# Two transformer blocks in fp32: the end of the expert stage rearranged (products of the return, the exit of the branch, the last norms, the output transfers)

## The chip, the cores and the metric

One core of one Trainium2 chip runs the whole program. The metric is the device time of one execution in microseconds (us); the figure for a kernel is the median of its runs. A profile is one further execution with its trace. In the trace PE is TensorE (matmuls), PEld its weight loads, DVE VectorE, ACT ScalarE, SP the engine that issues the transfers.

## The reference, cut to what matters

256 tokens of width 1024 go through a first block (two layers of attention) and a second block (two layers, l = 0 and 1, each attention plus a mixture of 16 experts). The change touches only the end of the second block's layers:

```python
N_EXPERTS, N_GROUPS, TOP_K, D_EXPERT = 16, 4, 2, 256
def moe_ffn(x, w_router, router_bias, w_gate, w_up, w_down):
    ...                                          # each token picks a group of 4 experts and 2 experts in it
    h = jax.nn.silu(jnp.einsum('nd,edf->enf', xt, w_gate)) * jnp.einsum('nd,edf->enf', xt, w_up)
    h = h * gates.T.astype(h.dtype)[:, :, None]
    y = jnp.einsum('enf,efd->nd', h, w_down)

def second_block(x, ...):
    for l in range(DEPTH):                       # DEPTH = 2
        h = jnp.einsum('bsd,dc->bsc', x, w_in[l])
        ...                                      # three kinds of attention, w_out, first layer_norm
        x = layer_norm(DEEPNORM_ALPHA * x + moe_ffn(x, ...), ln2_g[l], ln2_b[l])
    return x
```

## The kernel before

Everything is float32. A product of full precision is made of three matmuls in fp32r (`mm3`, L485 to L489): high by high, low by high, high by low part. ACT makes the high part of each quarter of weights (`act_cut`, L432) and DVE the low part (`dve_cut`, L440), in turn with their other work; SP loads the weights through a ring (L422). Each engine's instructions stand in the order in which `pe_...`, `act_...`, `dve_...`, `sp_...` functions write them, by hand; engines wait for each other by semaphores (`wait_ge`), which hold up all that stands behind them on the same engine.

**The experts.** The tokens lie in two tiles of 128 (i = 0, 1). If no group of experts has more than 128 tokens, a branch taken by PE, DVE, ACT and SP alike (`branch`, a compare and a jump) runs `pe_few`, `act_few`, `dve_few`; otherwise the `all` way stands behind it, over which a taken jump leads at the end. In the trace the `few` way ran in both layers. It gathers the tokens of each group g into 128 rows (xg), runs for e = 0 to 15 the products with gate and up weights (24 matmuls), the turn of the hidden rows (`turned`, 2 transposes) and the products with the down weights (`down`, 12 matmuls: first and second quarter k_, and in each the output halves n = 0 and 1, 3 matmuls each). Four experts of a group sum in banks 2*(g%2)+n; then ACT writes the high part of the group's output (`ys`, L2323, two halves) and DVE the low part (L2373). `back(i, g0, g1)` brings the rows of groups g0 to g1 back to the tokens of tile i: for each half n and each group two matmuls (L2263) of the one-hot matrix OHT with the high and the low part of ys. In program order PE does: up(15) with turned(14) inside, down(14), turned(15), `back(0, 1, 3)` (8 matmuls), down(15), `back(0, 3, 4)` (4), `back(1, 0, 4)` (16). `back(0, 0, 1)` stands before up(15).

**The end of a layer.** `dve_added` (L1583) adds the banks to X by halves and sums; L1584 makes the mean, `dve_middle` (L1590) the centred product with the gain, ACT the squares (L1607) and a first root by LN and EXP (L675, L676), `dve_root` (L681 to L685) refines it, `dve_scaled` (L1598) writes X. All this is done for tile 0 and then for tile 1. In layer 1 SP then writes out each tile with one transfer (L2210). In layer 0 PE transposes X of tile 0 (`pe_flip_x`, L1616, 8 transposes) still inside the branch, ACT (L1622) and DVE (L1628) write its high and low part hT; behind the branch PE starts the projection h10 of layer 1 tile by tile (`pe_proj_by_tiles`): 18 matmuls of tile 0, the transposes of X of tile 1, 6 more of tile 0, then 24 of tile 1. ACT and DVE, behind their own jump, first cut one more quarter of weights and then write hT of tile 1.

`att_bank` deals out PSUM banks 4 to 7 in rotation. `pe_idle(n, b)` (L496) issues n matmuls with a zero operand.

Of the kernel before, what the change touches and what calls it, by code (L numbers as in the profile page):

```python
# [125 lines left out]
def program(nc, t, out, cols, keep):  # L126
# [254 lines left out]
    first_turned, second_normed = sem("first_turned"), sem("second_normed")  # L381
# [13 lines left out]
    def write(pe, act, dve, pool, sp, branch):  # L395
# [1183 lines left out]
        def dve_added(i, key, ready):  # L1579
            sums, mean = small(2, "sums", i, *key), small(1, "mean", i, *key)  # L1580
            for c, x in enumerate(in_two(X[:, i, :])):
                dve.wait_ge(ready[c])
                dve.e.scalar_tensor_tensor(x, x, ALPHA, banks[2 * i + c].t[:, :], MUL, ADD, accum_out=sums[:, c:c + 1]).then_inc(*dve.did("added", *key, i, c))  # L1583
# [9 lines left out]
        def dve_scaled(i, key):  # L1593
# [16 lines left out]
        def pe_flip_x(i, name, src, ready):  # L1610
            for c, j0 in enumerate((0, 4)):
                b = att_bank(("xT", name, i, j0), (first_turned, c + 1) if name in (("few", 0), ("all", 0)) else at("xT", name, i, j0))
# [12 lines left out]
        def dve_flip_x(i, name):  # L1625
            for j0 in (0, 4):
                dve.wait_ge(at("high", "xT", name, i, j0))
                dve.e.tensor_tensor(hT[1][:, j0:j0 + 4, i * P:(i + 1) * P], bank_of["xT", name, i, j0].t[:, :].rearrange("p (j n) -> p j n", j=4),  # L1628
                                    hT[0][:, j0:j0 + 4, i * P:(i + 1) * P].bitcast(F32), SUB).then_inc(
                    *((first_turned, 1) if name in (("few", 0), ("all", 0)) else dve.did("xT", name, i, j0)))  # L1630
# [45 lines left out]
        def pe_mix_layer(l):  # L1676
            second = [at("added", "o1", 1, c) if l == 0 else (second_normed, c + 1) for c in range(2)]
# [386 lines left out]
        def pe_all(l):  # L2064
# [44 lines left out]
            pe_finish(l, way)  # L2109
# [78 lines left out]
        def pe_finish(l, way):  # L2188
            if l == 0:
                pe_flip_x(0, way, X, [at("x", *way, 0, c) for c in range(2)])  # L2190

        def act_finish(l, way):
            for i in range(2):
                act_add_and_norm(i, way)
                if l == 0 and i == 0:
                    act_flip_x(0, way)

        def dve_finish(l, way, ready):
            for i in range(2):
                dve_added(i, way, ready[i])  # L2200
                dve_middle(i, way, ln_loaded(l, 2))
                dve_scaled(i, way)
                if l == 0 and i == 0:
                    dve_flip_x(0, way)

        def sp_finish(l, way):
            if l == 1:
                for i in range(2):
                    sp.wait_ge(*[at("x", *way, i, c) for c in range(2)])
                    sp.e.dma_start(out[0, i * P:(i + 1) * P, :], X[:, i, :]).then_inc(d_out, 16)  # L2210
# [3 lines left out]
        def pe_few(l):  # L2214
# [23 lines left out]
            def down(e):  # L2238
                g, x = e // 4, e % 2
                for k_ in range(2):  # L2240
                    w = pe_quarter()
                    pe.wait_ge(at(*way, "gh", e))
                    for n in range(2):
                        b = banks[2 * (g % 2) + n]
                        first = e % 4 == 0 and k_ == 0
                        if first:
# [3 lines left out]
                                 first, e % 4 == 3 and k_ == 1)  # L2250
                    mm.then_inc(w_used, 1)
# [231 lines left out]
```

## Time and profile before

| | us |
|---|---|
| median of 3 runs | 1190.86 (1190.43 to 1192.14) |
| the profiled execution, its own time | 1189.19 |
| its span, first to last instruction | 1187.8 |
| PE busy in the span | 1120.8 (94%) |
| DVE busy / ACT busy | 901.4 (76%) / 737.3 (62%) |
| mean granted clock of TensorE | 0.983 |

The page of the profile counts each engine's busy time; the chain of work that ended last says which engine's work the end waited for. Times in the timeline are from the start of the span. The end of layer 0 lies at about 866 to 896 us, that of layer 1 at 1166 to 1187.8 us. A clock of 1.00 is 2.4 GHz, 0.50 is 1.2 GHz.

### The profile page before, as it was taken

How to read it: one execution, taken by the hardware profiler on the slowest of the kernel's cores; microseconds unless marked ns; L12 is line 12 of the kernel's file. 1: busy time of each engine (PE TensorE's matmuls, PEld its weight loads, DVE VectorE, ACT ScalarE, POOL GpSimd, SP SyncE). 2: the span in 40 equal slices, each digit the busy share in tenths (PEclk: the TensorE clock that was granted, in tenths of full speed). 3: DMA queues.
4: the chain of work that ended last, by engine and by line, in shares of the span. 5: the costliest groups of instructions: out<-in, count | busy, mean ns of one | idle time of the engine just before them, and what ended most of it. 6: DMA issues, size and time to landing. Idle time of an engine off the chain costs nothing.

```text
span 1187.8 us, 14609 instructions
## 1 busy us (share of the span) xinstructions
PE 1120.8 (94%) x5487; PEld 916.0 (77%) x5487; DVE 901.4 (76%) x1474; ACT 737.3 (62%) x1307; POOL 0.2 (0%) x4
## 2 busy tenths in 40 slices
PE   7799999999988999999999999999989999999996
PEld 5688887788777788878777777877768778787774
DVE  4756757677667867766578868999977886899996
ACT  5645565655556666566355554888845555488883
POOL 0000000000000000000000000000000000000000
PEclk9999999999999999998999998999989999999999
DMA  8554454443433455532542415999926331499991
GB/s 297 188 210 142 142 178 154 139 168 107 154 130 107 149 206 169 198 106 95 189 143 105 141 51 164 341 362 361 360 79 235 107 129 49 150 341 356 366 344 39
DMA packets 131554, 221.26 MB, mean 186 GB/s; under 512 B 6112, under 2 KB 77328, under 8 KB 131472
## 3 DMA queue, kind: packets, MB, share of 16 engines
q1 hardware_dynamic: 127632, 213.21, 52.7%
q10 hardware_dynamic: 3840, 6.98, 1.7%
q8 instruction: 47, 0.77, 0.3%
q14 instruction: 35, 0.29, 0.1%
HBM read 219.13 MB, written 1.05 MB: 185 GB/s over the span
## 4 chain that ended last, share of the span: by engine, by line
PE 75%; DVE 12%; ACT 8%; issue 3%; DMA 2%; DVEq 0%; ACTq 0%
PE bank L487 20%; PE bank L489 20%; PE bank L488 20%; PE bank L849 3%; PE bank L784 2%; ACT wH L432 2%; DVE wL L440 2%; ACT S L804 2%; PE bank L636 1%; DMA ring<-in_w_mem_kv 1%; DVE mx L793 1%; PE bank L830 1%; PE bank L2221 1%; PE bank L1765 1%; PE bank L1698 1%
## 5 line engine op out<-in xcount | busy, mean ns | idle before, releaser
L440 DVE TENSOR_TENSOR wL<-ring,wH 128x1024 fp32r<-128x1024 f32 (+1 forms) x316 | 375.5, 1213 | 143.6 <-ACT wH L432 142.7
L432 ACT ACTIVATE wH<-ring 128x1024 fp32r<-128x1024 f32 (+1 forms) x316 | 320.3, 1047 | 30.3 <-PE bank L489 14.9
L487 PE MATMUL bank<-wH,hTH 128*128 128x512 f32 (+2 forms) x592 | 238.8, 403 | 6.8 <-issue 3.0
L488 PE MATMUL bank<-wL,hTH 128*128 128x512 f32 (+2 forms) x592 | 232.6, 393 | 0.0
L489 PE MATMUL bank<-wH,hTL 128*128 128x512 f32 (+2 forms) x592 | 232.4, 393 | 0.0
L487 PEld LDWEIGHTS bank<-wH,hTH 128*128 128x128 f32 x592 | 112.1, 189 | 32.0 <-issue 5.6
L489 PEld LDWEIGHTS bank<-wH,hTL 128*128 128x128 f32 x592 | 111.8, 189 | 24.9
L488 PEld LDWEIGHTS bank<-wL,hTH 128*128 128x128 f32 x592 | 112.1, 189 | 23.1 <-issue 0.5
L487 PE MATMUL bank<-wH,xgH 128*128 128x512 f32 x256 | 104.7, 409 | 0.0
L488 PE MATMUL bank<-wL,xgH 128*128 128x512 f32 x256 | 101.2, 396 | 0.0
L489 PE MATMUL bank<-wH,xgL 128*128 128x512 f32 x256 | 101.2, 395 | 0.0
L804 ACT ACTIVATE S<-bank,sm 128x256 f32<-128x256 f32 (+1 forms) x144 | 59.5, 428 | 62.4 <-DVE sm L797 62.2
L487 PEld LDWEIGHTS bank<-wH,xgH 128*128 128x128 f32 x256 | 48.1, 188 | 12.1 <-DVE wL L440 2.6
L555 ACT ACTIVATE qkv<-bank,factors 128x512 f32<-128x512 f32 x50 | 33.6, 689 | 38.0 <-PE bank L489 37.9
L489 PEld LDWEIGHTS bank<-wH,xgL 128*128 128x128 f32 x256 | 48.1, 188 | 11.5
L488 PEld LDWEIGHTS bank<-wL,xgH 128*128 128x128 f32 x256 | 48.2, 188 | 9.5
L487 PE MATMUL bank<-wH,gh 128*128 128x512 f32 x128 | 51.1, 399 | 0.1
L488 PE MATMUL bank<-wL,gh 128*128 128x512 f32 x128 | 50.6, 395 | 0.0
L489 PE MATMUL bank<-wH,gh 128*128 128x512 f32 x128 | 50.6, 395 | 0.0
L440 DVE TENSOR_TENSOR wL<-ring_G,wH 128x1024 fp32r<-128x1024 f32 x40 | 48.5, 1221 | 1.3 <-ACT wH L432 1.0
L440 DVE TENSOR_TENSOR wL<-ring_K,wH 128x1024 fp32r<-128x1024 f32 x40 | 48.3, 1219 | 1.5 <-ACT wH L432 1.4
L836 ACT ACTIVATE PT<-bank 128x512 f32<-128x512 f32 x44 | 25.4, 599 | 33.3 <-PE bank L830 33.3
(292 smaller groups left out, 1868.3 us busy)
## 6 DMA issues: line engine op xcount, KB each, us to landing
ring<-in_w_in_a SPq DMA_DIRECT2D x44, 1024.0 KB, 5.1
ring<-in_w_out SPq DMA_DIRECT2D x20, 1024.0 KB, 4.9
ring<-in_w_down SPq DMA_DIRECT2D x20, 1024.0 KB, 6.3
ring<-in_w_gate SPq DMA_DIRECT2D x36, 512.0 KB, 5.2
ring<-in_w_up SPq DMA_DIRECT2D x36, 512.0 KB, 6.7
ring<-in_w_in_b SPq DMA_DIRECT2D x14, 1024.0 KB, 5.1
ring<-in_w_mem_kv SPq DMA_DIRECT2D x8, 1024.0 KB, 7.0
ring<-in_w_in SPq DMA_DIRECT2D x8, 1024.0 KB, 5.5
```

The lines of the kernel that those rows point to most:

```text
L432: act.e.activation(quarter_parts(q)[0], quarter_in_ring(q), COPY).then_inc(w_high, 1)
L440: dve.e.tensor_tensor(lo, quarter_in_ring(q), hi.bitcast(F32), SUB).then_inc(w_low, 1)
L487: pe.e.matmul(o, a[0], b[0], start=first, stop=False)
L488: pe.e.matmul(o, a[0], b[1], start=False, stop=False)
L489: return pe.e.matmul(o, a[1], b[0], start=False, stop=last)
L555: act.e.activation(dst(i), bank_of["proj", name, i].t[:, 0:slab_w[name]], COPY, scale=factor(key)[:, i:i + 1] if key else 1.0).then_inc(*a ...
L636: tr = pe.e.transpose(o, src(i, j), ident)
L784: mm = pe.e.matmul(score_bank(u, s // each)[:, s % each, :], u.qh(s)[:, i * P:(i + 1) * P], u.kh(s)[:, k:k + n], start=u.mask is None, sto ...
L793: dve.follow().tensor_reduce(u.mx[:, each * x:each * x + each], score_bank(u, x), AX, MAX).then_inc(*dve.did())
L804: act.e.activation(u.S[:, s, 0:n], score_bank(u, s // each)[:, s % each, :], EXP, bias=nb[:, s:s + 1], scale=u.scale, accum_out=u.den[:, s ...
L836: act.e.activation(u.PT[:, kt, :, :].rearrange("p h q -> p (h q)"), bank_of["turn", u.name, kt].t[:, :], COPY).then_inc(*act.did("PT", u.n ...
L849: mm = pe.e.matmul(b.t[:, s * u.dv:(s + 1) * u.dv], u.PT[:, kt, s, :], u.vh(s, kt), start=kt == 0, stop=kt == u.nk - 1)
```

## The change

1. In `pe_few` tile 1 no longer uses banks 2 and 3, which hold the sums of group 3, but two banks of the rotation (6 and 7, which `turn["att"] = 3` at e = 15 arranges). So `back(1, ...)` is cut up: `back(1, 0, 2)` (8 matmuls) ahead of turned(15), `back(1, 2, 3)` (4) behind down(15), `back(0, 3, 4)` and `back(1, 3, 4)` (4 each) after it.
2. The last group of matmuls for half n = 0 of down(15) signals ("first half"), and ACT starts on that half of ys before the other one is done. The matmul with the high part of ys waits for ACT alone (`ys_high`), the one with the low part for DVE.
3. In layer 0 PE ends its branch with 10 matmuls by zero and transposes X of tile 0 behind the jump. Since both ways of the branch use it, it waits for a new semaphore `first_normed`. The same work of ACT and DVE stays inside the branch.
4. In layer 1 DVE adds both tiles, then does both middles, one refinement of the root with two columns, and four scalings; ACT does the squares of both tiles and one LN and EXP.
5. The output goes out in four transfers of a half tile (256 KB) instead of two of a tile (512 KB).

```diff
-                if key[-1] == 0 and i == 1:
-                    mm.then_inc(second_normed, 1)
+                if key[-1] == 0:
+                    mm.then_inc((first_normed, second_normed)[i], 1)
...
         def pe_mix_layer(l):
+            if l:
+                turn["att"] = 3
+                pe_flip_x(0, "exit", X, [(first_normed, 1), (first_normed, 2)])
...
-        def pe_finish(l, way):
-            if l == 0:
-                pe_flip_x(0, way, X, [at("x", *way, 0, c) for c in range(2)])
         def act_finish(l, way):
+            if l:
+                ss = small(2, "ss2", *way)
+                for i in range(2):
+                    act.wait_ge(at("mean", i, *way))
+                    act.follow().activation(squares[:, :], X[:, i, :], SQUARE, bias=small(1, "mean", i, *way), accum_out=ss[:, i:i + 1]).then_inc(*act.did("sum", "ln", *way))
+                act_root(("ln", *way), ss, 2, 1.0 / D, "eps5")
+                return
...
+        def dve_finish(l, way, ready, sums_in=(None, None)):
+            if l:
+                for i in range(2):
+                    dve_added(i, way, ready[i], sums_in[i])
+                for i in range(2):
+                    dve_middle(i, way, ln_loaded(l, 2))
+                dve.wait_ge(at("sum", "ln", *way))
+                r = dve_root(("ln", *way), small(2, "ss2", *way), 2, 1.0 / D, "eps5")
+                ...
+                return
...
-                    sp.e.dma_start(out[0, i * P:(i + 1) * P, :], X[:, i, :]).then_inc(d_out, 16)
+                    for c in range(2):
+                        sp.wait_ge(at("x", *way, i, c))
+                        sp.e.dma_start(out[0, i * P:(i + 1) * P, c * 512:(c + 1) * 512], X[:, i, c * 512:(c + 1) * 512]).then_inc(d_out, 16)
...
+                        if e == 15 and k_ == 1 and n == 0:
+                            mm.then_inc(*pe.did(*way, "first half", e))
...
             def back(i, g0, g1):
                 for n in range(2):
-                    b = banks[2 * i + n]
                     if g0 == 0:
-                        pe.wait_ge(b.free, at(*way, "OHT", i))
-                        b.free = at("added", *way, i, n)
+                        if i:
+                            b = att_bank((*way, "back", 1, n), at("added", *way, i, n))
+                        else:
+                            b = bank_of[(*way, "back", 0, n)] = banks[n]
+                            ...
...
-                        pe.wait_ge(at(*way, "ys", g, n))
                         for x in range(2):
+                            pe.wait_ge(at(*way, "ys" if x else "ys_high", g, n))
...
+                if e == 15:
+                    back(1, 0, 2)
             turned(15)
             back(0, 1, 3)
             down(15)
+            back(1, 2, 3)
             back(0, 3, 4)
-            back(1, 0, 4)
-            pe_finish(l, way)
+            back(1, 3, 4)
+            if l == 0:
+                pe_idle(10, att_bank((*way, "idle"), None))
```

PE from the end of down(14) to turned(15) in layer 0, of before: ys_137 to ys_140 are groups 1 and 2, T_67 the hidden rows.

```order
L489 MATMUL bank<-wH_102,gh_144 128x512
L2235 MATMUL bank<-const,T_67 128x128 x2
L2263 MATMUL bank<-ys_137,OHT 128x512
L2263 MATMUL bank<-ys_138,OHT 128x512
L2263 MATMUL bank<-ys_139,OHT 128x512
```

And of after, where ys_135 and ys_136 are group 0:

```order
L489 MATMUL bank<-wH_102,gh_144 128x512
L2301 MATMUL bank<-ys_135,OHT 128x512
L2301 MATMUL bank<-ys_136,OHT 128x512
L2301 MATMUL bank<-ys_137,OHT 128x512
L2301 MATMUL bank<-ys_138,OHT 128x512
L2301 MATMUL bank<-ys_135,OHT 128x512
L2301 MATMUL bank<-ys_136,OHT 128x512
L2301 MATMUL bank<-ys_137,OHT 128x512
L2301 MATMUL bank<-ys_138,OHT 128x512
L2266 MATMUL bank<-const,T_67 128x128 x2
```

Eight matmuls for tile 1 moved ahead of turned(15), so ahead of down(15) too. DVE at the end of layer 1, of before:

```order
L1583 SCALAR_TENSOR_TENSOR X,sm<-X,bank 128x512 x2
L1584 TENSOR_SCALAR sm<-sm 128x1
L1590 SCALAR_TENSOR_TENSOR middle_86<-X,sm,lnw 128x512 x2
L681 TENSOR_SCALAR sm<-sm 128x1
L683 SCALAR_TENSOR_TENSOR sm<-sm 128x1
L684 TENSOR_TENSOR sm<-sm 128x1
L685 SCALAR_TENSOR_TENSOR sm<-sm 128x1
L1598 SCALAR_TENSOR_TENSOR X<-middle_86,sm,lnw 128x512 x2
```

and the same eight once more for tile 1. Of after, for both tiles:

```order
L1583 SCALAR_TENSOR_TENSOR X,sm<-X,bank 128x512 x2
L1584 TENSOR_SCALAR sm<-sm 128x1
L1590 SCALAR_TENSOR_TENSOR middle_86<-X,sm,lnw 128x512 x2
L1590 SCALAR_TENSOR_TENSOR middle_87<-X,sm,lnw 128x512 x2
L681 TENSOR_SCALAR sm<-sm 128x2
L683 SCALAR_TENSOR_TENSOR sm<-sm 128x2
L684 TENSOR_TENSOR sm<-sm 128x2
L685 SCALAR_TENSOR_TENSOR sm<-sm 128x2
L2227 SCALAR_TENSOR_TENSOR X<-middle_86,sm,lnw 128x512 x2
L2227 SCALAR_TENSOR_TENSOR X<-middle_87,sm,lnw 128x512 x2
```

where L1583 and L1584 stand twice ahead of the middles; four instructions of one column went.

## Rows read from the trace of the kernel before

**Rows 1.** Page, part 4: shares of the span on the last chain, by engine

```profile
PE 75%; DVE 12%; ACT 8%; issue 3%; DMA 2%; DVEq 0%; ACTq 0%
```

**Rows 2.** Chain that ended last, end of layer 1: start us, us, what

```profile
1166.51 1.86 PE bank L2263 x8
...
1171.21 0.61 ACT ys L2323
1171.84 0.70 DVE ys L2373
...
1172.58 0.74 PE bank L2263 x2
...
1173.35 1.31 DVE X L1583 x4
...
1177.36 1.42 DVE X L1598 x2
1178.78 1.22 DVE X L1583 x4
...
1180.27 1.43 DVE middle L1590 x2
```

**Rows 3.** Timeline, end of layer 1: start us, us, engine, line

```profile
1172.58 4.98 PE L2263 MATMUL bank<-ys,OHT 128*128 128x512 f32 x20 [1.41 <-DVE ys L2373]
...
1178.85 5.83 SPq L2210 DMA_DIRECT2D out<-X  x2
...
1182.84 1.41 DVE L1598 SCALAR_TENSOR_TENSOR X<-middle,sm,lnw 128x512 f32<-128x512 f32 x2
```

**Rows 4.** DMA issues, 1170 to 1188 us: KB each, median us to landing

```profile
out<-X SPq DMA_DIRECT2D x2, 512.0 KB, 3.0
```

**Rows 5.** Timeline, layer 0, around the start of down(15)

```profile
866.99 2.11 PE L2263 MATMUL bank<-ys,OHT 128*128 128x512 f32 x8
...
868.60 0.42 DVE L2362 TENSOR_TENSOR gh<-bank,gh 128x256 fp32r<-128x256 f32 x1
...
869.17 0.47 PE L487 MATMUL bank<-wH,gh 128*128 128x512 f32 x1
```

**Rows 6.** Timeline, layer 0, across the exit of the branch

```profile
879.19 1.32 PE L1616 MATMUL bank<-const,X 128*128 128x128 f32 x8 [0.63 <-DVE X L1598]
...
883.52 0.69 PE L487 MATMUL bank<-wH,hTH 128*128 128x416 f32 x1 [3.02 <-issue]
...
887.61 0.90 ACT L432 ACTIVATE wH<-ring 128x832 fp32r<-128x832 f32 x1 [2.45 <-issue]
...
888.76 1.03 DVE L440 TENSOR_TENSOR wL<-ring,wH 128x832 fp32r<-128x832 f32 x1 [1.57 <-ACT wH L432]
...
889.20 1.03 PE L1616 MATMUL bank<-const,X 128*128 128x128 f32 x8
...
890.46 1.29 DVE L1628 TENSOR_TENSOR hTL<-bank,hTH 128x512 fp32r<-128x512 f32 x2 [0.68 <-ACT hTH L1622]
...
891.21 0.46 PE L487 MATMUL bank<-wH,hTH 128*128 128x416 f32 x1
...
895.86 0.37 PE L487 MATMUL bank<-wH,hTH 128*128 128x452 f32 x1
```

**Rows 7.** Busy time by stretch: us, busy of each engine, granted clock, DMA share, GB/s

```profile
882.00:889.00 7.00, 5.48 (x17) 5.29 (x18) 4.99 (x14) 2.64 (x5) 0.00 (x0) 0.55 0.03 6
...
1005.00:1014.00 9.00, 9.00 (x34) 7.67 (x34) 5.29 (x18) 4.38 (x7) 0.00 (x0) 0.50 0.18 73
```

**Rows 8.** Queues of the transfers, 880 to 882 us: packets, MB, share of 16 engines

```profile
q8 instruction: 1, 0.02, 3.6%
```

**Rows 9.** Timeline, entry of layer 0's branch: zero products and what follows

```profile
716.31 3.76 PE L496 MATMUL bank<-zeroR,identR 128*128 128x512 f32 x8
...
717.02 0.14 DVE L2038 CAST count<-sm 1x1 int32<-1x1 f32 x1
...
719.86 2.35 PE L2221 MATMUL bank<-OH,xs 128*128 128x512 f32 x7
```

More of the change, by code:

```diff
@@ L1611, in pe_flip_x @@
             for c, j0 in enumerate((0, 4)):
-                b = att_bank(("xT", name, i, j0), (first_turned, c + 1) if name in (("few", 0), ("all", 0)) else at("xT", name, i, j0))
+                b = att_bank(("xT", name, i, j0), (first_turned, c + 1) if name == "exit" else at("xT", name, i, j0))
                 pe.wait_ge(ready[c])
@@ L1628, in dve_flip_x, with act_flip_exit, dve_flip_exit @@
                 dve.e.tensor_tensor(hT[1][:, j0:j0 + 4, i * P:(i + 1) * P], bank_of["xT", name, i, j0].t[:, :].rearrange("p (j n) -> p j n", j=4),
-                                    hT[0][:, j0:j0 + 4, i * P:(i + 1) * P].bitcast(F32), SUB).then_inc(
-                    *((first_turned, 1) if name in (("few", 0), ("all", 0)) else dve.did("xT", name, i, j0)))
+                                    hT[0][:, j0:j0 + 4, i * P:(i + 1) * P].bitcast(F32), SUB).then_inc(*dve.did("xT", name, i, j0))
+        def act_flip_exit(way):
+            for j0 in (0, 4):
+                act.wait_ge(at("turned", "xT", "exit", 0, j0))
+                act.e.activation(hT[0][:, j0:j0 + 4, 0:P], bank_of["xT", "exit", 0, j0].t[:, :].rearrange("p (j n) -> p j n", j=4),
+                                 COPY).then_inc(*act.did("high", "exit", way, j0))
+        def dve_flip_exit(way):
+            for j0 in (0, 4):
+                dve.wait_ge(at("high", "exit", way, j0))
+                dve.e.tensor_tensor(hT[1][:, j0:j0 + 4, 0:P], bank_of["xT", "exit", 0, j0].t[:, :].rearrange("p (j n) -> p j n", j=4),
+                                    hT[0][:, j0:j0 + 4, 0:P].bitcast(F32), SUB).then_inc(first_turned, 1)
         def dve_rotate(src, dst, n, w, c, s, *name, scratch=T0):
@@ L2320, in down @@
                     g = e // 4
-                    act.wait_ge(at(*way, "down", e), at(*way, "gathered", 7))
+                    act.wait_ge(at(*way, "gathered", 7))
                     for n in range(2):
+                        act.wait_ge(at(*way, "first half", e) if e == 15 and n == 0 else at(*way, "down", e))
                         act.e.activation(ys[g][0][:, n * 512:(n + 1) * 512], banks[2 * (g % 2) + n].t[:, :], COPY).then_inc(*act.did(*way, "ys_high", g, n))
@@ L2393, in dve_few @@
             down(15)
-            dve_finish(l, way, [[at(*way, "back", i, n) for n in range(2)] for i in range(2)])
+            dve_finish(l, way, [[at(*way, "back", i, n) for n in range(2)] for i in range(2)],
+                       [[bank_of[(*way, "back", i, n)] for n in range(2)] for i in range(2)])
         def experts(l):
```

31 lines of the change are left out of this document (19 added, 12 removed).

## The prediction, written before the changed kernel ran

> **What bounds the kernel.** I read the page's shares of the last chain first: the end waits for PE in three quarters of the span [rows 1]. Next the chain by time around the two ends of a layer, since the change touches nothing else: there the work that is waited for goes from PE over ACT and DVE to DVE alone [rows 2]. Last the timeline of those places, for what lies beside the chain.
>
> Three readings carry the rest. (a) In the last expert PE has no gap: eight products of the return fill 1.86 us of the chain, ahead of down(15) [rows 2]. (b) Behind down(15) PE is not what the end waits for. Its 20 products run from 1172.58 to 1177.56 [rows 3], but DVE adds tile 1 only at 1178.78, when it is through with tile 0 [rows 2]. (c) In layer 0 PE starts h10 at 883.52, 3.02 us after its last transpose, with nothing to wait for but its jump [rows 6]. Yet the 24 products of tile 1 wait for hT of tile 1, whose first low part DVE writes from 890.46 on; they start at 891.21 [rows 6].
>
> **Part 1, products pulled ahead.** Eight products of tile 1 come from behind down(15), where PE had time (b), to a place ahead of it, where it has none (a). Price in layer 1: +1.86 us on everything behind. In layer 0 down(15) started at 869.17, while the eight products ahead of it, begun at 866.99, were issued by 868.85; the 0.32 between was a wait for DVE's low part of the hidden rows, 868.60 to 869.02 [rows 5]. That wait is covered now, as its inputs move by 1.86 too but DVE is free sooner than that: +1.86 - 0.32 = +1.54. What it buys is that tile 1 is ready for DVE soon after tile 0, which only part 4 uses.
>
> **Part 2, the half signal.** Before, ACT started at the end of the last product (1171.21), DVE 0.63 later, PE at 1172.58, DVE's add at 1173.35, that is 2.14 us in all [rows 2]. Now half n = 0 is signalled three products earlier, 3 x 0.233 (1.86 / 8) = 0.70. ACT's first half is over when the last product ends, DVE's low part of it 0.65 later. ACT's second half cannot start before that last product, so DVE's second low part ends at 1.31 + 0.04. PE meanwhile issues back(1, 2, 3), four products, until 0.76; its pair for half 0 goes at 0.76 and 0.99, and the add, which followed the pair's start by 0.77 before [rows 2], can start at 1.5. Gain 2.14 - 1.5 = 0.65 us in either layer. If ACT or DVE were not free then, the gain would be 0; in layer 0 they have two more quarters of weights to cut, but these end at about 872.3 and the half signal comes at 873.0.
>
> So the first add moves by +1.86 - 0.65 = +1.2 in layer 1 and +1.54 - 0.65 = +0.9 in layer 0.
>
> **Part 3, the exit of layer 0.** PE's last real product now starts at about 873.7 + 2.4 = 876.1 (last expert's end 872.2 + 1.54, then the pairs above and four more). Ten zero products at 0.25 (4.98 / 20, [rows 3]) last to 878.7. X of tile 0 is there at 879.19 + 0.9 = 880.1. The jump cost at least the 3.02 us of PE's idle time and at most 883.52 - 879.85 = 3.6, counted from the start of the last four transposes. At 880.75 the trace has one packet of 16 KB on a queue named instruction [rows 8]: PE fetches code. If the jump is taken while the zero products still run, PE is back by 876.2 + 3.6 = 879.8, in time. For that speaks the entry of layer 0: the count was written at 717.16, zero products ran from 716.31 to 720.07, and the first product of the branch followed at 719.86 with no gap, with PE's reading of the count and its branch between [rows 9]. Value taken: 0, bounds 0 and +1.9 (878.7 + 3.3 - 880.1, jump behind the last zero product).
> The Trainium skill ("Runtime: NRT & Kernel Launch", Instruction fetch mechanics) says that a taken branch to a target outside the fetched window stalls until the page is brought; the trace's 16 KB packet and the 3 us agree. Its "Advanced Engine Details and Errata" (Engine Queue Depths) gives TensorE a queue of 64: by that all zero products fit behind one another and the jump is reached in time; without such a queue the sum would be 1.9 us higher.
>
> What does PE's earlier start bring? h10 starts when the first low part of tile 0 is there, 881.2 + 0.9 = 882.1 instead of 883.52, and perhaps at full clock: from 882 to 889 the granted clock was 0.55 [rows 7], after PE had stood still. But both are hidden. Tile 1's products wait for DVE, and DVE for ACT: ACT comes out of its own jump at 887.61, cuts a quarter (0.90), DVE cuts it at 888.76 (1.03), and only then writes hT [rows 6]. ACT's jump follows the last root of tile 1, which moved by +0.9. So ACT is back at 888.5, DVE's cut starts at 889.65 and ends at 890.7, and tile 1's low part starts there instead of 890.46. Before, 0.67 us went between DVE's cut and its low part on PE's late transposes (889.20) and ACT; now X of tile 1 is turned by 889. Sum for layer 0: +0.9 - 0.67 = **+0.2**. If the cover by ACT were not there, PE's gain of 1.4 would show.
>
> **Part 4, one root for both tiles.** From the first add to the end of the last scaling DVE took 1173.35 to 1184.25 = 10.9 us, that is per tile 1.49 for add and mean, 1.43 middle, 1.1 root, 1.42 scaling [rows 2, 3]. Now the root stands once (-1.1), and its ACT part is over while DVE does the four middles (-0.2), with 0.1 less where like instructions follow each other. Tile 1's banks are ready at about 2.9 after down(15), its first add comes at 3.0: no wait. Gain **1.4**, bounds 1.1 and 1.6.
>
> **Part 5, output by halves.** The last transfer was 512 KB and landed 3.0 us after issue [rows 4]. The last one is now 256 KB; at some 410 GB/s its data take 0.64 us less, and the three ahead of it are issued 0.7 us apart, as DVE's scalings end. Issue by SP takes some 0.4 us each, less than that. Gain **0.64**; bounds 0 (a transfer's length is all fixed cost, or the halves queue up) and 1.0.
>
> **Sum.** Layer 0: +0.2. Layer 1: +1.86 - 0.65 - 1.4 - 0.64 = -0.83. Together -0.6 us. Against the profiled execution, 1187.8 of span and 1.4 around it, that is 1189.19 - 0.6 = 1188.6; that execution lies 1.7 below the median, so the forecast is 1190.86 - 0.6 = **1190.2**.
>
> **Rivals.**
> *PE comes late out of its branch.* The jump is taken only behind the zero products, so PE's transposes, and behind them ACT, DVE and the whole of tile 1, come up to 1.9 us later: 1192.1. For it: PE's idle time of 3.02 begins at the end of its transposes, not before [rows 6]. Against it: [rows 9]. It decides as soon as PE is back later than 880.1.
> *The clock falls ahead of tile 1, slower than before.* PE now stands still in smaller pieces, about 885.6 to 887.5 (waiting for X of tile 1) and 890 to 891.4 (for hT). The clock of 0.55 before came behind such a stillness [rows 7]. If it falls there, the 24 products that took 891.21 to 895.86 [rows 6] take up to 4.6 us more, I say 3.7: 1190.2 + 3.7 = 1193.9. It decides if the granted clock is 0.50 beyond 891.4. Against it: six products and eight transposes lie between, and PE is busy from 882.1 on.
> *The clock around layer 1's router.* From 1005 to 1014 PE was fully busy at clock 0.50 [rows 7], worth up to 4.5 us, about half of it on the chain, since DVE's small instructions follow. Nothing in the change is meant for it, but the stretches in which PE stands still ahead of it move by some tenths: if the clock stays up there, -2.5: 1187.7.
> *The half signal does nothing*, since ACT's second half and PE's order decide the add anyway: +0.65 in layer 1 and nearly so in layer 0: 1191.4.
>
> **Numbers.** Forecast 0.60, late exit 0.12, clock ahead of tile 1 0.08, router's clock 0.12, half signal idle 0.08. The range takes in the forecast with its bounds (0.2 - 1.6 - 1.0 and the like give -1.9 to +1.2), the late exit and the idle half signal, and leaves out the two of the clock, 0.2 together: 1188.2 to 1192.6. A measurement of this kernel can tell about 0.2% or 2.4 us from no change: faster than 1188.5 is the router's clock and a tail of the forecast, 0.14; slower than 1193.2 the clock ahead of tile 1 and a tail of the late exit, 0.10; within, 0.76.
>
> **What would show it.** Right: down(15) of layer 1 ends 1.9 us later against down(14), ACT's ys starts before the last product of down(15), add of tile 0 at +1.2; one 128x2 root; last transfer lands in about 2.4 us; in layer 0 PE's transposes follow X of tile 0 by 0.1 us and the wait stands behind them, h10's tile 1 at +0.2. Wrong: a gap of PE between zero products and transposes that X does not explain; PE idle ahead of down(15) that swallows the eight products, then the gain is up to 3 us more; a 256 KB transfer that takes 3.0 us.

## The result, and the profile after

| | before | after |
|---|---|---|
| median, us | 1190.86 | 1196.94 |
| lowest and highest of 20 runs each | 1188.04, 1197.33 | 1192.58, 1200.56 |
| ratio, 95% interval | | 1.0045 [1.0033, 1.0056] |
| span of the profiled execution | 1187.8 | 1196.5 |
| mean time of TensorE at half clock, by the runs' granted clock | 48 | 60 |

The change made the kernel 5.4 us slower by the ratio (6.1 by the medians). The forecast was 1190.2 and its range ended at 1192.6, so the measured time lies outside it. (The last row is (1 - clock) x 2 x time, averaged over the timed runs; "before" there stands for the 35 runs beside the first experiments.)

**Where the 8.7 us between the two profiled spans are.** Both traces are cut at the same events: the start of the return of group 0 in layer 0 (`back(0, 0, 1)`, 857.3 before, 860.45 after), DVE's first add of layer 0, the first product of h11 (the projection that follows h10 in layer 1), the first product of layer 1's router, its first gather, DVE's first add of layer 1, the end.

| stretch | before | after | difference | forecast |
|---|---|---|---|---|
| start to the return of group 0, code that is unchanged | 857.3 | 860.4 | +3.1 | 0 |
| to the first add, layer 0 (parts 1, 2) | 17.1 | 17.8 | +0.8 | +0.9 |
| to h11 (part 3) | 21.5 | 22.7 | +1.2 | -0.7 |
| h11 to the router | 104.1 | 108.9 | **+4.8** | 0 |
| router to the first gather | 18.6 | 18.5 | -0.1 | 0 |
| to the first add, layer 1 (parts 1, 2) | 154.8 | 155.8 | +1.1 | +1.2 |
| to the end (parts 4, 5) | 14.4 | 12.3 | -2.1 | -2.0 |

The first row is a matter of single executions (before's profile lay 1.7 us under its median, after's 1.0 over): its clock fell in other places, and more often, in the first 400 us. The last two rows came as worked out. What went wrong lies in rows three and four.

The chain that ended last, end of layer 1 of the changed kernel (start us, us, what), beside [rows 2]:

```profile
1176.03 1.85 PE bank L2301 x8
1177.88 0.22 PE bank L2266 x2
1178.10 1.86 PE bank L2301 x8
...
1182.75 1.40 PE bank L2301 x6
1184.17 1.32 DVE X L1583 x4
1185.72 1.22 DVE X L1583 x4
1187.18 2.66 DVE middle L1590 x4
...
1191.47 2.07 DVE X L2227 x3
```

Two blocks of eight products stand in the chain instead of one (part 1's price, 1.86), both adds and then four middles follow each other, and one root fills the 1.6 us ahead of L2227. Timeline of ACT there, and below it the DMA issues of 1180 to 1198 us (KB each, median us to landing), beside [rows 2 to 4]:

```profile
1182.09 1.30 ACT L2368 ACTIVATE ys<-bank 128x512 fp32r<-128x512 f32 x2 [3.57 <-PE bank L489]
...
1188.49 0.30 ACT L675 ACTIVATE sm<-sm,const 128x2 f32<-128x2 f32 x1
```

```profile
out<-X SPq DMA_DIRECT2D x4, 256.0 KB, 2.4
```

ACT starts on ys 0.66 us ahead of the last product's end (1182.75), the root has two columns, and the median of the four transfers lands in 2.4 us where that of the two larger ones took 3.0 [rows 4].

The exit of layer 0 (the end of its branch and the start of h10 behind it), timeline of PE, ACT and DVE of the changed kernel, beside [rows 6]:

```profile
860.45 1.09 PE L2301 MATMUL bank<-ys,OHT 128*128 128x512 f32 x4
...
879.57 2.35 PE L496 MATMUL bank<-zeroR,identR 128*128 128x512 f32 x10
883.12 1.32 PE L1616 MATMUL bank<-const,X 128*128 128x128 f32 x8 [1.20 <-DVE X L1598]
885.28 0.43 PE L487 MATMUL bank<-wH,hTH 128*128 128x416 f32 x1 [0.84 <-DVE hTL L1642]
...
890.51 1.32 PE L1616 MATMUL bank<-const,X 128*128 128x128 f32 x8 [1.60 <-DVE X L1598]
893.63 0.46 PE L487 MATMUL bank<-wH,hTH 128*128 128x416 f32 x1 [1.80 <-DVE wL L440]
...
894.88 0.50 PE L487 MATMUL bank<-wH,hTH 128*128 128x416 f32 x1
895.17 0.55 PE L488 MATMUL bank<-wL,hTH 128*128 128x416 f32 x1
...
898.52 0.35 PE L489 MATMUL bank<-wH,hTL 128*128 128x416 f32 x1
```

```profile
878.30 0.69 DVE L1583 SCALAR_TENSOR_TENSOR X<-X,bank 128x512 f32<-128x512 f32 x1
...
891.43 0.90 ACT L432 ACTIVATE wH<-ring 128x832 fp32r<-128x832 f32 x1 [2.34 <-issue]
...
892.55 1.02 DVE L440 TENSOR_TENSOR wL<-ring,wH 128x832 fp32r<-128x832 f32 x1 [1.43 <-ACT wH L432]
893.49 1.28 DVE L1628 TENSOR_TENSOR hTL<-bank,hTH 128x512 fp32r<-128x512 f32 x2
```

PE is out of its jump in time: what it waits for at 883.12 is X. h10 starts 7.0 us behind the first add (878.30) where it was 9.2 before, as meant, and this gains nothing: PE then stands still twice, 1.60 and 1.80 us, and the second wait ends with DVE's cut of the weights behind ACT's jump, in the order that the forecast had. Then the clock falls amid tile 1: products of 416 columns follow each other by 0.35 us from 895.17 on, and by 0.19 again from 898.5. Windows of the changed kernel (us, busy of PE, PEld, DVE, ACT, POOL, granted clock, DMA share, GB/s), beside [rows 7]:

```profile
882.00:889.00 7.00, 4.95 (x26) 4.14 (x26) 6.00 (x14) 2.84 (x6) 0.00 (x0) 1.00 0.01 2
...
895.10:898.50 3.40, 3.40 (x11) 3.28 (x11) 1.93 (x4) 0.96 (x1) 0.00 (x0) 0.52 1.00 342
...
942.00:953.00 11.00, 9.90 (x64) 8.45 (x62) 9.19 (x30) 7.16 (x18) 0.00 (x0) 1.00 0.25 98
953.00:967.00 14.00, 13.82 (x39) 10.33 (x40) 9.44 (x26) 5.96 (x22) 0.00 (x0) 0.51 0.01 2
```

From 882 to 889 the clock is now 1.00 where it was 0.55 [rows 7]; instead it is 0.52 from 895.1 to 898.5, and 0.51 for 13.7 us from 953.1 on, in the attention of layer 1, where the kernel before had 1.00. The old fall, from 881.5 to 888.5, cost next to nothing: until 883.52 PE was in its jump, and tile 0's products, slow from there on, were covered by ACT and DVE but for the 0.67 us by which the transposes came late, which part 3 of the prediction had booked. The two new falls lie on work that the end waits for. PE in the attention of layer 1, changed kernel, and below it the kernel before:

```profile
950.70 1.97 PE L849 MATMUL bank<-qkv,PT 128*128 128x64 f32 x16 [0.99 <-ACT PT L836]
952.50 0.39 PE L1797 MATMUL bank<-const,G 128*128 128x128 f32 x2
953.18 1.12 PE L941 MATMUL bank<-const,Y 128*128 128x128 f32 x4 [0.29 <-DVE Y L856]
...
954.66 2.07 PE L784 MATMUL bank<-kT,qT 64*128 64x128 f32 x8
```

```profile
945.59 1.97 PE L849 MATMUL bank<-qkv,PT 128*128 128x64 f32 x16 [0.99 <-ACT PT L836]
947.39 0.39 PE L1781 MATMUL bank<-const,G 128*128 128x128 f32 x2
948.07 0.66 PE L941 MATMUL bank<-const,Y 128*128 128x128 f32 x4 [0.29 <-DVE Y L856]
...
948.89 1.16 PE L784 MATMUL bank<-kT,qT 64*128 64x128 f32 x8
```

The waits are the same to the hundredth (0.99 and 0.29); only behind them the same eight products take 2.07 us and not 1.16. So the loss at this place is no new wait.

### The profile page after: what moved, and what is told of

It is laid out like the page before. It is cut to its first block, busy times and chain, and to the rows that moved or that the text cites. A ratio compares the mean times of both kernels' runs of the same rounds, so it can differ in the third digit from the quotient of the medians.

```text
span 1196.5 us, 14623 instructions
## 1 busy us (share of the span) xinstructions
PE 1131.9 (95%) x5497; PEld 927.1 (77%) x5497; DVE 900.8 (75%) x1470; ACT 737.1 (62%) x1305; POOL 0.2 (0%) x4
## 4 chain that ended last, share of the span: by engine, by line
PE 76%; DVE 11%; ACT 8%; issue 2%; DMA 2%; ACTq 0%; DVEq 0%
PE bank L487 20%; PE bank L489 20%; PE bank L488 20%; PE bank L849 3%; PE bank L784 3%; ACT wH L432 2%; DVE wL L440 2%; ACT S L804 2%; PE bank L636 2%; DMA ring<-in_w_mem_kv 1%; PE bank L830 1%; DVE mx L793 1%; PE bank L2301 1%; PE bank L2252 1%; PE bank L1781 1%
```

## The experiments

Each run is compared with runs of the kernel before made beside it on the same chip. The kernel before had medians from 1190.28 to 1191.84 on these chips, so where two changed kernels are compared, the difference of their ratios (times 1191 us) counts, and that of their medians stands beside it. The intervals reach 0.0015 to 0.0025 to either side of the ratio, 2 to 3 us. An edit is shown against the changed kernel, or against the kernel that the heading names; `...` marks lines left out. "Low" is the mean time at half clock of the timed runs, with that of before behind the stroke. My theory after the result: the new exit carries the loss, locally by its clock fall in h10, and beyond by the fall in the attention that goes with it. First, which part it is.

**e1_noexit: part 3 undone, all else kept.**

```diff
         def pe_mix_layer(l):
-            if l:
-                turn["att"] = 3
-                pe_flip_x(0, "exit", X, [(first_normed, 1), (first_normed, 2)])
...
             if l == 0:
-                pe_idle(10, att_bank((*way, "idle"), None))
+                turn["att"] = 3
+                pe_flip_x(0, way, X, [at("x", *way, 0, c) for c in range(2)])
```

> The changed kernel with the old exit of layer 0: PE transposes X of tile 0 inside the branch again, no zero products behind the return; products ahead, half signal, one root and output by halves stay. Theory A (the exit did it: tile 1 of h10 comes later, and TensorE's clock now falls to 1.2 GHz inside or behind h10, where it used to fall ahead of it): back to before's time less the end of layer 1, 1190 to 1191. Theory B (the eight products pulled ahead and what they delay cost it): stays 1195 to 1197. Theory C (any change of timing at the exit of layer 0 shifts where the clock falls in the attention of layer 1): about 1193, with a mean clock that tells the time.

Measured: 1191.28 beside 1191.84, ratio 1.0001 [0.9985, 1.0017], low 51 / 48. Without the new exit nothing of the loss is left, in time or in the profile (104.1 us from h11 to the router, with no fall in the attention).

**e2_exitonly: the kernel before with part 3 alone** (the lines above, the other way round).

> The kernel before with part 3 alone: ten zero products end PE's branch in layer 0, X of tile 0 is transposed behind the jump. Theory A: 1195 to 1197, clock 0.975, as the changed kernel or a little above it, since the end of layer 1 gains nothing here. Theory B: 1189.5 to 1191. Theory C: about 1193.

Measured: 1194.20 beside 1191.84, 1.0025 [0.9999, 1.0050], low 49 / 48. In its profile h11 starts 24.0 us behind the first add (21.5 before) with a fall at 892.6, and none follows in the attention (104.1 us from h11 to the router). In its profile the exit costs its local 2.5 us by itself, and the further loss in the attention does not follow. Its runs differ more than any other's: ten lie from 1190 to 1196, two at 1204 and 1205, and these two had 77 and 80 us at half clock where the ten had 33 to 50.

**e3_endonly: the kernel before with parts 4 and 5 alone.**

```diff
                 if e == 15:
-                    back(1, 0, 2)
...
-            back(1, 2, 3)
             back(0, 3, 4)
-            back(1, 3, 4)
+            back(1, 0, 4)
```

> The kernel before with parts 4 and 5 alone: in layer 1 one root for both tiles and four output transfers; products of tile 1 stay behind down(15) in banks 2 and 3, no half signal, old exit. All theories: the stretch behind down(15) shortens. Tile 1's 16 products end 4.9 us after the first pair, its add waits for them some 2 us; so root -1.4 becomes about 0, transfer -0.64: 0.5 to 1 us less than before, 1190, with the clock as before.

Measured: 1192.16 beside 1191.84, 1.0002 [0.9987, 1.0017], low 51 / 48: no gain where the sum had 2.0. In its profile the stretch from the first add of layer 1 to the end takes 14.8 us, against 14.4 before and 12.3 to 12.7 in every kernel that has these parts and also pulls products ahead. So part 4 needs part 1: DVE now turns to tile 1 as soon as its first add is done, and there PE's 20 products are what it waits for, 0.91 and 1.12 us in this run's timeline:

```profile
1180.69 0.69 DVE L1583 SCALAR_TENSOR_TENSOR X<-X,bank 128x512 f32<-128x512 f32 x1 [0.91 <-PE bank L2297]
...
1182.51 0.69 DVE L1583 SCALAR_TENSOR_TENSOR X<-X,bank 128x512 f32<-128x512 f32 x1 [1.12 <-PE bank L2297]
```

Reading (b) held for the old order of DVE alone.

**e4_pullhalf: the kernel before with parts 1 and 2 alone.**

```diff
         def act_finish(l, way):
-            if l:
-                ss = small(2, "ss2", *way)
...
-                return
```

> The kernel before with parts 1 and 2 alone: eight products of tile 1 ahead of down(15), the half signal; old exit, old end of layer 1. By my sum +0.9 in layer 0 and +1.2 in layer 1: 1193. Theory B: 1195 to 1197. Theory A: 1193 with before's clock. Theory C: 1193 to 1196 with a lower clock.

Measured: 1193.91 beside 1191.84, +2.1 by the medians and +1.8 by the ratio, 1.0015 [0.9998, 1.0032], low 54 / 48. The sum had +1.2 for parts 1 and 2 in layer 1 and +0.9 in layer 0. The time agrees, but its interval just takes in no change, and 6 us more of low clock can make up most of it. The profile shows the parts more surely: from the return of group 0 to the first add it takes 0.8 us more in layer 0 and 1.0 in layer 1.

**e5_keep and e6_idle0: the changed kernel with more, or without, zero products.** e5 puts seven ahead of and seven behind the transposes of X of tile 1 inside h10, where PE stands still for 1.60 and 1.80 us; e6 takes away the ten ahead of the jump.

```diff
-            pe_proj_by_tiles(f"h{l}0", lambda: pe_flip_x(1, l, X, second))
+            def amid():
+                if l:
+                    pe_idle(7, banks[4])
+                pe_flip_x(1, l, X, second)
+                if l:
+                    pe_idle(7, banks[4])
+            pe_proj_by_tiles(f"h{l}0", amid)
```

```diff
-                pe_idle(10, att_bank((*way, "idle"), None))
+                pass
```

> The changed kernel with seven zero products ahead of the transposes of X of tile 1 inside h10 and seven behind them, in PE's two waits of 1.6 and 1.8 us there; the work itself is as before. Clock theory (the new exit moves the fall of the clock from PE's wait ahead of h10, where it costs nothing, to tile 1 of h10 and further, where each us at 1.2 GHz costs): no fall in 885 to 900 us, 2 to 4 us less than the changed kernel: 1193 to 1195, mean clock 0.978 to 0.981. Placement theory (the moved products and the jump themselves cost it): 1197, unchanged, or some tenths more.

> The changed kernel with no zero products at the end of PE's branch; the transposes of tile 0 still stand behind the jump. Clock theory: PE stands still longer ahead of h10, the clock falls there again, where it is hidden by ACT and DVE, and is back for tile 1: 1193 to 1195. Rival (the zero products help, by holding the clock and hiding the jump): 1198 to 1199.

Measured: e5 1192.07 beside 1191.74, 1.0006 [0.9987, 1.0024], low 46 / 49: 4.6 us under the changed kernel by the ratios (4.9 by the medians), with nothing but zero products added. Two windows of its profile, tile 1 of h10 and the attention:

```profile
895.00:902.00 7.00, 7.00 (x37) 6.62 (x36) 3.40 (x4) 5.83 (x18) 0.00 (x0) 1.00 1.03 373
950.00:964.00 14.00, 13.46 (x75) 10.81 (x76) 11.46 (x29) 7.05 (x24) 0.00 (x0) 1.00 0.01 2
```

Both late falls are gone. One of 3.4 us stands at 883, in tile 0 of h10 and 5 us ahead of the first added zero product, so this one profile does not show that the zeros alone moved the falls; for them speaks that e6 had a fall at the same place and kept both late ones. e6: 1193.51, 1.0015 [0.9997, 1.0033], low 51 / 49; its profile still has the falls in h10 and in the attention (108.8 us from h11 to the router), and yet half of its runs lie under 1194. Its time is what the clock theory expected, its profile is not: the fall ahead of h10 came (882.5), and the later ones stayed. So the ten zero products are not needed for these falls.

**e7_l1pull and e8_l1pull_exit.** In e7 layer 0 pulls nothing ahead and has the old exit, but keeps the half signal; layer 1 has all of the change. e8 is e7 with the new exit.

```diff
                 if e == 15:
-                    back(1, 0, 2)
+                    if l:
+                        back(1, 0, 2)
...
-            back(1, 2, 3)
+            if l:
+                back(1, 2, 3)
             back(0, 3, 4)
-            back(1, 3, 4)
+            back(1, 3 if l else 0, 4)
```

> A version meant to keep what helps: in layer 0 the products of tile 1 stay behind down(15) and the old exit stays, with the half signal; layer 1 has all of the change (products ahead, half signal, one root, output by halves). By my sum layer 0 -0.6 and layer 1 -0.8: 1.4 less than before, 1190.4; against the changed kernel with the old exit (1191.3) 1.5 less, since the eight products no longer delay layer 0's last down product.

> As the version before it in this call, but with the new exit of layer 0 (ten zero products, transposes of tile 0 behind the jump). Its difference from that one is the exit alone, without the pulled products in layer 0. Clock theory: 2.5 to 5 us more, 1193 to 1195, with a mean clock not higher. If the exit costs only together with the pulled products: 1190.5 to 1191.5.

Measured: e7 1190.84, 1.0004 [0.9988, 1.0020], low 56 / 49; e8 1195.67, 1.0048 [1.0030, 1.0065], low 58 / 49. The exit costs 5.2 us here by the ratios (4.8 by the medians), in the profiles 2.5 us ahead of h11 and 4.7 in the attention, less 1.3 in the router.

**e9_attkeep: the changed kernel with four zero products in the wait of 0.99 us in the attention.** (This expectation and that of e10 measure to a product of the router that comes 2.8 us later than the one of my table: their 106.9 and 111.7 are the table's 104.1 and 108.9.)

```diff
                 if n == 3:
                     pe_flip(("qT3", l), chunk(HR), 4, [at("queries", l)])
+                if n == 4 and l:
+                    pe_idle(4, banks[4 + (turn["att"] + 1) % 4])
```

> The changed kernel with four zero products more (512 columns each), in layer 1 alone, behind the transposes of the last latent unit in the attention, where PE stood still for 0.99 us at 949.7 until ACT had copied PT. In the trace of the changed kernel the granted clock fell 3.4 us behind that wait, at 953.1, for 13.7 us, and the stretch from the first product of h11 to the router of layer 1 took 111.70 us where 106.93 stood before. Theory (the clock is lost there because PE stands still, and half of the lost time is paid): the fall at 953 is gone, the stretch is 106.9 to 107.2, the stretch from the last half signal of layer 0 to h11 keeps its 40.7 with its fall at 895, and the time is 4 to 5 us under the changed kernel, 1192 to 1193. Rival (the 4.7 us are another delay, of a transfer or of ACT, and the clock's fall only goes with it): the stretch stays near 111.7, and the time at 1196 to 1197.

Measured: 1194.13 beside 1190.28, 1.0030 [1.0008, 1.0051], low 51 / 44: by the ratios 3.6 us over before, against 5.4 for the changed kernel, and the two intervals overlap. The 4 to 5 us that were expected did not come. Three windows, the attention, 4 us later, and the router:

```profile
945.00:965.00 20.00, 19.22 (x120) 15.83 (x119) 16.61 (x48) 10.11 (x38) 0.00 (x0) 1.00 0.10 41
969.00:976.00 7.00, 6.35 (x19) 4.70 (x18) 4.30 (x14) 4.06 (x12) 0.00 (x0) 0.51 1.09 371
1006.00:1026.00 20.00, 18.91 (x69) 16.26 (x68) 14.35 (x41) 6.75 (x12) 0.00 (x0) 0.52 0.15 55
```

The fall at 953 is gone, but the clock fell at 969 instead (h11 to the router 106.5 us, between 104.1 and 108.9), and in the router it stayed low for 20.5 us, not 10.2 (21.4 us from the router to the first gather; 18.5 in the changed kernel). In the profile, where one place was covered, part of the loss stood at the next.

**e10_shift and e12_noexit_shift: lateness alone.** Eight zero products (1.9 us) between h10 and h11 of layer 1, in the kernel before (e10) and in e1, the changed kernel with the old exit (e12).

```diff
             pe_proj_by_tiles(f"h{l}0", lambda: pe_flip_x(1, l, X, second))
+            if l:
+                pe_idle(8, banks[4 + (turn["att"] + 1) % 4])
```

> The kernel before with eight zero products (8 x 0.235 = 1.9 us of PE) put into layer 1 between the slabs h10 and h11, and nothing else: the exit of layer 0 is the old one, with its fall of the clock at 881.5, and all that stands behind it comes 1.9 us later, as in the changed kernel. Theory A (the fall of the clock in the attention of layer 1 follows from the later start alone, since what the clock does depends on when PE's still stretches come): a fall near 952, the stretch from h11 to the router 111.7, the time 1191.8 + 1.9 + about 4.7 = 1198. Theory B (it follows from what PE did before, the fall inside h10 or the zero products of the new exit, and not from the lateness): no fall there, the stretch 106.9, and the time 1191.8 + 1.9 = 1193.7.

> The changed kernel with the old exit of layer 0 (part 3 undone, its ten zero products with it), and with eight zero products (1.9 us of PE) in layer 1 between the slabs h10 and h11: all other parts of the change, and the lateness that the new exit gave h11, without the new exit. Theory A (the lateness is enough: PE's still stretches in the attention of layer 1 then meet the clock as they did in the changed kernel): 1191.3 (the same kernel without the eight) + 1.9 + 2 to 4 = 1195 to 1197, the mean time at half clock near the changed kernel's 60 us. Theory B (the new exit itself is needed: its zero products and the transposes and products behind it keep the clock up where the old exit lost it in a wait, and it is lost later where it costs): 1191.3 + 1.4 to 1.9 = 1193, the mean at half clock about 50 us.

Measured: e10 1191.63 beside 1190.28, 1.0011 [0.9994, 1.0029], low 45 / 44. e12 (six runs) 1199.14 beside 1191.52, 1.0052 [1.0033, 1.0072], low 67 / 46, over e1 by 6.1 us by the ratios and 7.9 by the medians. Windows in the attention, e10 and then e12:

```profile
949.00:959.00 10.00, 10.00 (x29) 7.19 (x28) 7.25 (x18) 3.53 (x15) 0.00 (x0) 0.50 0.01 2
```

```profile
952.00:966.00 14.00, 13.85 (x39) 10.36 (x40) 9.41 (x26) 5.94 (x22) 0.00 (x0) 0.52 0.01 2
```

Both have the fall, and neither has the new exit. e12 has all that I put down to the exit: 108.5 us from h11 to the router, and more low clock than the changed kernel itself. So the new exit is not needed for it: theory A for e12. e10 speaks against theory A by its time: over its own before it has +1.3 us, where A had 6.6 and theory B 1.9, and its interval takes in B and shuts out A. Its profile has the fall that A expected (107.1 us from h11 to the router), but its router came out 1.2 us shorter (17.4 against 18.6), and its timed runs had no more low clock than before's. The same 1.9 us of zero products cost 1.3 in one kernel and 6.1 in the other.

**e11_router, e13_after_router, e14_nopull_router: the clock held in the router.** In both layers' router, six zero products more; e11 is e7 with them, e13 the whole changed kernel with them, e14 parts 2, 4 and 5 with them (no products ahead, old exit).

```diff
             for i in range(2):
+                if i:
+                    pe_idle(2, banks[4 + (turn["att"] + 1) % 4])
                 pe_flip_x(i, ("router", l), middle[i], [at("middle", f"p{l}", i, c) for c in range(2)])
+                pe_idle(2, banks[4 + (turn["att"] + 1) % 4])
                 b = banks[i]
```

> A version that might beat both kernels: layer 0 with its products where the kernel before has them, the old exit and the half signal, layer 1 with all of the change, and in the router of both layers six zero products more (two behind the transposes of each tile, two behind the logits of tile 0). In the run of that version without them the clock fell at 1005.9 for 17.1 us in the router of layer 1, where PE has only products of 16 columns; the second tile's 16 products took 3.44 us there against 1.96 for the first's. Theory (the small products do not hold the clock, zero products would): the fall goes or gets shorter, 3 to 4 us come back in layer 1 for about 0.9 us of zero products on the path, and less in layer 0: 1190.8 - 2 to -3 = 1188 to 1189. Rival (the clock falls later instead, in the stretch of zero products and gathers behind): 1190.8 + 1 to 1.5 = 1192.

> The changed kernel, all of it, with six zero products more in the router of each layer (two behind the transposes of each tile, two behind the logits of tile 0), as they gave 3.5 us in the version with layer 0 undone. Theory (what the clock costs in the router is a cost by itself, whatever the exit does): 1196.9 - 3 to -3.5 = 1193.5, still over the kernel before, since the new exit's 2 us in h10 and the fall in the attention stay. Rival (the chip has so much low clock to give, and what is covered in one place comes back in another): 1196 to 1197, with the mean time at half clock unchanged near 60 us.

> A second version that might beat both: the half signal, one root for both last tiles and the outputs by halves, no products pulled ahead in either layer, the old exit, and the six zero products in each router. It differs from the run that had 1187.35 only in layer 1, where that one pulled the products ahead. Theory (the pull costs 1.5 to 1.9 us in a layer, since down(15) comes later by eight products and nothing waits less for it): 1187.35 - 1.5 = 1185.9. Rival (in layer 1 the products ahead let the second tile end earlier and pay for themselves): 1187 to 1188.

| | us | before beside it | ratio, 95% | low |
|---|---|---|---|---|
| e11 | 1187.35 | 1190.28 | 0.9983 [0.9966, 1.0001] | 36 / 44 |
| e13 | 1188.85 | 1191.52 | 0.9982 [0.9963, 1.0001] | 33 / 46 |
| e14 | 1187.83 | 1191.52 | **0.9967 [0.9952, 0.9982]** | 33 / 46 |

PE in layer 1's router, changed kernel, and then e13, with two windows of e13 (h11's start and the router):

```profile
1012.88 2.25 PE L1781 MATMUL bank<-wr,xT 128*128 128x16 f32 x16 [0.25 <-ACT xT L1882]
...
1016.74 3.59 PE L1781 MATMUL bank<-wr,xT 128*128 128x16 f32 x16
1020.17 3.76 PE L496 MATMUL bank<-zeroR,identR 128*128 128x512 f32 x8
```

```profile
1006.93 1.93 PE L1784 MATMUL bank<-wr,xT 128*128 128x16 f32 x16
...
1010.54 1.93 PE L1784 MATMUL bank<-wr,xT 128*128 128x16 f32 x16
1012.33 1.99 PE L496 MATMUL bank<-zeroR,identR 128*128 128x512 f32 x8
```

```profile
895.00:902.00 7.00, 7.00 (x38) 6.79 (x37) 4.20 (x6) 4.34 (x13) 0.00 (x0) 1.00 1.02 377
...
1003.00:1014.00 11.00, 11.00 (x83) 10.03 (x81) 9.25 (x24) 7.17 (x17) 0.00 (x0) 1.00 0.03 4
```

The second tile's 16 products take 1.93 us instead of 3.59, and the stretch from router to first gather 16.8 instead of 18.5 in spite of 1.4 us of zero products. Between the profiles of e7 and e11 that stretch went from 19.8 to 16.6 us; by the ratios the two kernels differ by 2.5 us (by the medians 3.5, of which 1.5 lies between the chips). In e14 it took 18.1 us, hardly less than the 18.6 before: the second tile's products ran at full clock there too, but 6.8 us of low clock stand at 1013, in the small and the zero products behind them. And e2, without zero products, has no fall in the first 12 us of its router, so a profile alone does not show that the zeros hold the clock; the timed runs' low clock (33 to 36 us with them, 44 to 67 without) is the stronger sign. e13 gained 7.5 us (by the ratios) on the changed kernel, where 3 to 3.5 were expected, and the rest does not lie in layer 1's router: h11 starts 21.3 us behind the first add (22.7), and the attention takes 104.1 us (108.9). Neither is touched by the edit. With the six zero products of layer 0's router, 170 us ahead, the fall at the exit had another place: 885.5, amid tile 0, under the cover of ACT and DVE. The rival, that low clock comes back elsewhere, is refuted: 33 us instead of 60. e14 is faster than the changed kernel and than before, and is the only one whose interval lies clear of before. Against e11 it is no better than the intervals can tell (by the medians 3.7 under its before against 2.9), as its rival said: from the return of group 0 in layer 1 to the end both profiles take 30.5 us (31.2 before). The products ahead cost e11 some 2 us up to the first add and give them back behind it, 12.7 us against 14.6.

## Why the prediction was wrong, point by point

- **Reading (a) and part 1** held: a second block of eight products, 1.85, stands in layer 1's chain. First add of layer 0 +0.8 against +0.9, of layer 1 +1.1 against +1.2. That the sum of parts 1 and 2 is so near is in part luck: part 2 alone is worth 0.90 us and not 0.65 (return of group 0 to the first add, layer 0 of e7, e11 and e14 and layer 1 of e14, against before), and so part 1 cost 1.7 and 2.0 where the sum had 1.54 and 1.86.
- **Part 2** held in its way: ACT's ys starts 0.66 ahead of the end of down(15), forecast 0.70.
- **Part 3, the jump**, held: PE was back before X. Of the +0.9 - 0.67 for tile 1 only 0.26 of the 0.67 came: its first product stands 16.58 us behind the first add (16.84 before), which itself came 0.79 later, together +0.5 and not +0.2. DVE's low part did come 0.9 us sooner behind the first add (893.49 - 878.30 against 890.46 - 874.37). But the last six products of tile 0 wait for DVE's cut too (893.63), and tile 1 stands behind them; before, PE started these six at 889.99, 0.2 us after the cut was done. The forecast overlooked this second tie.
- **Parts 4 and 5** held in size, -2.1 against -2.0, and each by itself: from the first add to the end of the last scaling 9.37 us instead of 10.90 (forecast -1.4), behind that 2.95 instead of 3.52 (forecast -0.64). But they hold only together with part 1 (e3), which the prediction names as their condition without a price for the pair: it is worth 1.86 - 2.1, nearly nothing.
- **The step that failed** is in part 3, "But both are hidden", and the sum that follows from it, which has no term for the clock in the stretches that nobody touched. The prediction saw the clock of 0.55 from 882 to 889 [rows 7], called the waste hidden and took it that a change of it would be hidden too. In the changed kernel the clock is 1.00 there, and low for 3.4 us in tile 1 of h10 and for 13.7 us in the attention, where it costs. These two, 1.4 + 4.8 us, turn the forecast -0.6 into a loss of the size measured. The rival "the clock falls ahead of tile 1" named this, with 0.08. Of its price of 3.7 us only 1.4 came (tile 1 took 6.09 us instead of 4.65), since the fall lasted 3.4 us. The fall in the attention of layer 1, 4.8 us, stands in no rival.
- **The rivals.** Late exit and idle half signal are refuted by the rows above. The router's clock did not get better in the changed kernel (10.2 us low in both profiles); what it was worth of that stretch, 1.7 us in e13, 3.2 in e11 and 0.5 in e14, lies around the 2.5 that the rival said.
- **The range** of -2 to +2.4 around the forecast was made of errors of single steps, and its working does not come out: the bounds of parts 4 and 5 give -1.2 to +0.3 us against before, not -1.9 to +1.2. The runs of the kernel before alone spread over 9 us, from 1188 to 1197, and inside one set of them the time rises by 0.24 to 0.32 us for each us at half clock. The 12 us more of low clock in the changed kernel are worth 3 to 4 by that, of the 6 between forecast and measurement; the rest that slope does not give. A shift of the kind that any edit makes should have carried that term.

The Trainium skill ("TensorE: Matmul & The Clock Gate", What's actually happening) says that the chip judges PE's activity on a timer that runs free of the program, so that one kernel can come out differently from run to run. The traces agree so far: the waits of 0.99 and 0.29 us in the attention are the same in both kernels, with clock 1.00 behind them in one and 0.51 in the other. The Trainium skill ("TensorE: Matmul & The Clock Gate", HAM oscillation) takes half of the time at low clock as its price. Here the runs of the kernel before show 0.24 to 0.32 of it; that the rest lies in waits is argued, not shown.

**What stays open.** That 1.9 us of zero products ahead of h11, with PE busy on both sides of them, can bring the fall in the attention and a loss of 6.1 us is shown (e12 against e1, one edit). That it is the lateness, and which lateness, is open: e2's h11 was the latest of all behind the return of group 0 (41.1 us) and had no fall there; e10's had one and paid nearly nothing in its timed runs. Why the new exit brings the two falls is open in the same way. Each kernel has one profile, and the falls were seen in that one only. That e13's zero products in layer 0's router changed the places behind is argued from the order in time; no experiment had them alone.

## What to carry to other kernels

Before removing a wait of PE, ask in which waits the clock falls now and where the next candidate stands if it does not fall there; a fall in a wait can be nearly free, and stretches of small products or short waits that nobody touched can pay for it. Give every edit that moves a tuned kernel by a microsecond or two the spread of the clock in its range, and look for time at half clock in the timed runs, not in one profile. A few zero products where PE has only small work (six in a router: 1.4 us spent, 0.5 to 3.2 us gained net in that stretch in three profiles) can be worth more than the shortening of a chain.

## What was unexpected of the hardware

- Falls of the granted clock lasted from 3.4 to 20.5 us in the traces, and the same stretch of the program had one of 10.2 us in one kernel, 17.1 in another and 20.5 in a third (router of layer 1: before, e7, e9).
- In the router PE was busy without a gap, 9.00 of 9.00 us, at clock 0.50 [rows 7]; with six zero products among the same instructions it was busy 11.00 of 11.00 us at 1.00 (e13).
- 1.9 us of zero products, with nothing else changed, cost 1.3 us in one kernel (e10) and 6.1 us in another (e12); six of them in each router gained 7.5 us on the whole changed kernel (e13).
